# Seven block products in place of eight for the last 8 of the 44 up chunks of a two-layer fp32 transformer kernel

## Chip, cores and metric

One core of one Trainium2 chip runs the whole program once. The metric is the device time of one execution in microseconds, the median of the runs; lower is better. Engine names in the rows: PE is TensorE, PEld its weight loads, DVE VectorE, ACT ScalarE, POOL GpSimd, SP the engine that issues the loads.

## What is computed

Two decoder layers over 512 tokens of width 1024, all in fp32. The change concerns the feed-forward part of the first layer (D_FF is 2816, so `w_up` has 5632 columns, 44 chunks of 128):

```python
def causal_dwconv(x, w, b):            # K = 3 taps over the tokens
    xp = jnp.pad(x, ((0, 0), (K - 1, 0), (0, 0)))
    y = b + xp[:, 0:S] * w[0]
    for j in range(1, K):
        y = y + xp[:, j:j + S] * w[j]
    return y

def conv_ffn(x, w_up, conv_w, conv_b, w_down):
    u = causal_dwconv(x @ w_up, conv_w, conv_b)
    g, val = jnp.split(u, 2, axis=-1)
    return (jax.nn.gelu(g) * val) @ w_down
```

After it come a layer norm, a second layer of mixers and an MLP (`m1`, 1024 to 4096, squared ReLU, and `m2` back).

## The kernel before

**Products.** Each fp32 operand is split into a high and a low half (`whi`, `wlo` for weights, `xh`, `xl` for activations), and each product is three matmuls: high by high, high by low, low by high. A *chunk* is 128x1024 weights (512 KB). Chunks of all weight matrices form one list (`WEIGHTS`, `CHUNKS`): 44 `up` chunks, then 34 `down` chunks, and so on. For each chunk SP loads it into one of 4 `stage` buffers (`NSTAGE`), ACT casts it to `whi`, and DVE subtracts to get `wlo`; the pair lies in one of 7 slots (`NSPLIT`) until PE has used it. A stage buffer is loaded again once the `wlo` of its chunk is done. This is the step `split`; `pump` issues as many as there are slots.

**Order.** A class `Plan` writes one list of steps at build time. Each engine walks that list and issues its own part of each step, in that order; nothing overtakes on an engine. Semaphores count finished work (`mm` chunks multiplied, `w_lo` chunks split, `up_y`, `up_t`, `up_c`, `up_h` stages of the up block, `combined` and `taken` the terms of the block products).

**Up, before.** A plain `up` chunk is 24 matmuls of 512 columns. Chunk `j` is half `r = j % 2` (0 gate, 1 value) of pair `c = j // 2`. ACT copies the bank into `U` (shifted by two tokens) and writes the third tap with the bias (L2234, L2237); DVE adds the other two taps (L2863, L2866); for the gate ACT applies gelu (L2241); for the value DVE multiplies both (L2874) into `hid1`.

**Seven products.** `down`, `m2` and part of `m1` are multiplied in 2x2 blocks with seven products in place of eight (Winograd's form). The products are named `r1`, `r2`, `t11`, `r3`, `t12`, `r4`, `t22`. For `m1`, which computes features as `up` does, a *group* replaces four plain chunks by seven products, each of 24 matmuls of 256 columns. Its sums of activations (`r1` to `r4`) are made once, three of them kept in split slots (so 4 of the 7 slots are left for weights while groups run). The sums of weights (`a` to `d`) are made in DRAM by transfers of GpSimd, 1 MB each, one after the other, each released by a count of chunks (`at(n)` in `add_up`). Between the products of a group come small operations: ACT copies the bank of `r2` (`taken`), DVE makes `v` = that minus `t11`, `w` = `v` plus `r1`, ACT writes `w` back into a bank (`seed`) before `r4` is added there, and DVE makes `c22` and `c21` before `t22` is added. The waits of a product on these:

```python
                if kind == "t12":
                    q.wait_ge(S["combined"], plan.combined_at["m1", "v", g])
                elif kind == "r4":
                    q.wait_ge(S["taken"], plan.copied_at["m1", "seed", g])
                elif kind == "t22":
                    q.wait_ge(S["combined"], plan.combined_at["m1", "c21", g])
```

**Up to down.** The first `down` products need activations made from `hid1`: `x_from("down", k)` is a cast on ACT (`xh`, L2012) and a subtraction on DVE (`xl`, L2525). Those for k = 1 to 3 wait until the first half of chunk 43 is multiplied, those for k = 4 to 6 until `up` is done. A `down` chunk is 12 matmuls of 512 columns.

## Time and profile before

| | us |
|---|---|
| median of 3 runs | 1231.41 (1231.21 to 1232.08) |
| the profiled execution | 1231.81 |
| its span in the trace | 1230.0 |
| PE busy | 1222.7 (99%) |
| DVE busy | 899.3 (73%) |
| ACT busy | 652.9 (53%) |

The span is that of the first to the last instruction; 1.8 us of the profiled time lie outside it. Busy time of PE is modelled from pipelined matmuls, which overlap in the rows (a matmul of 512 columns has a duration of 389 ns, and the next starts 227 ns after it), so a time per chunk is read from starts, not from durations. The same holds for short operations of DVE and ACT, whose next one starts some 0.1 us before the end of the last.

### The profile page before, as it was taken

What the parts mean: (1) busy time and instruction counts of PE and PEld (TensorE: products, weight loads), DVE (VectorE), ACT (ScalarE), POOL (GpSimd) and SP (SyncE); (2) the same over time, 40 slices, a digit from 0 to 9 for tenths busy, and PEclk for the clock granted to TensorE, in tenths of its full rate; (3) what the DMA queues carried; (4) which work ended last, traced back from release to release, by engine and by line L of the source; (5) the groups of instructions that cost most, each with busy time, mean ns of one, the idle gap of its engine ahead of it and who ended that gap; (6) DMA issues with size and microseconds to landing.
All of it is one profiled execution on the core that took longest, in us unless ns stands there. A gap on an engine that the chain in (4) does not pass through costs nothing.

```text
span 1230.0 us, 17180 instructions
## 1 busy us (share of the span) xinstructions
PE 1222.7 (99%) x6662; PEld 1050.5 (85%) x6662; DVE 899.3 (73%) x1281; ACT 652.9 (53%) x1078; POOL 56.0 (5%) x80
## 2 busy tenths in 40 slices
PE   9999999999999999999999999999999999999998
PEld 9887898898889888888888899778898999988886
DVE  6778888576568656555588587887687777887886
ACT  5565654244546444444465464669354544665654
POOL 0000012000000000000000000000000000000000
PEclk9999999999999999999999999999999999999999
DMA  8445478837635787878676429776736789776562
GB/s 296 150 139 192 161 265 226 283 116 210 185 107 188 209 236 208 198 241 202 212 246 181 139 69 259 207 194 191 248 104 159 265 271 265 256 220 190 173 213 78
DMA packets 63976, 244.53 MB, mean 199 GB/s; under 512 B 6900, under 2 KB 14580, under 8 KB 54424
## 3 DMA queue, kind: packets, MB, share of 16 engines
q1 hardware_dynamic: 53096, 167.55, 40.6%
q0 software_dynamic: 10368, 75.50, 24.9%
q8 instruction: 53, 0.87, 0.3%
q10 hardware_dynamic: 432, 0.39, 0.1%
q14 instruction: 27, 0.22, 0.1%
HBM read 235.55 MB, written 81.26 MB: 258 GB/s over the span
## 4 chain that ended last, share of the span: by engine, by line
PE 99%; DMA 0%; DVE 0%; ACT 0%; issue 0%; DVEq 0%
PE bank L1509 15%; PE bank L1510 15%; PE bank L1511 15%; PE bank L1713 6%; PE bank L1715 6%; PE bank L1714 6%; PE bank L1740 3%; PE bank L1741 3%; PE bank L1739 3%; PE bank L1654 2%; PE bank L1658 2%; PE bank L1653 2%; PE bank L1656 2%; PE bank L1655 2%; PE bank L1657 2%; PE bank L1790 1%
## 5 line engine op out<-in xcount | busy, mean ns | idle before, releaser
L2491 DVE TENSOR_TENSOR wlo<-stage,whi 128x1024 fp32r<-128x1024 f32 (+1 forms) x276 | 332.8, 1212 | 113.5 <-ACT whi L1973 112.4
L1509 PE MATMUL bank<-xh,whi 128*128 128x512 f32 (+1 forms) x944 | 339.4, 360 | 0.2 <-issue 0.2
L1510 PE MATMUL bank<-xl,whi 128*128 128x512 f32 (+1 forms) x944 | 335.5, 355 | 0.0
L1511 PE MATMUL bank<-xh,wlo 128*128 128x512 f32 (+1 forms) x944 | 335.5, 355 | 0.0
L1973 ACT CAST whi<-stage 128x1024 fp32r<-128x1024 f32 (+1 forms) x276 | 284.9, 1039 | 78.5 <-PE bank L1715 27.3
L1509 PEld LDWEIGHTS bank<-xh,whi 128*128 128x128 f32 x944 | 178.5, 189 | 29.9 <-issue 5.3
L1511 PEld LDWEIGHTS bank<-xh,wlo 128*128 128x128 f32 x944 | 178.5, 189 | 25.1
L1510 PEld LDWEIGHTS bank<-xl,whi 128*128 128x128 f32 x944 | 178.6, 189 | 24.4 <-issue 0.2
L1715 PE MATMUL bank<-whi,xl 128*128 128x512 f32 x328 | 127.7, 389 | 0.0
L1714 PE MATMUL bank<-wlo,xh 128*128 128x512 f32 x328 | 127.7, 389 | 0.0
L1713 PE MATMUL bank<-whi,xh 128*128 128x512 f32 x328 | 127.7, 389 | 0.0
L1715 PEld LDWEIGHTS bank<-whi,xl 128*128 128x128 f32 x328 | 61.6, 188 | 12.8
L1714 PEld LDWEIGHTS bank<-wlo,xh 128*128 128x128 f32 x328 | 61.6, 188 | 12.8
L1713 PEld LDWEIGHTS bank<-whi,xh 128*128 128x128 f32 x328 | 61.6, 188 | 12.7
L2863 DVE SCALAR_TENSOR_TENSOR R<-R,par 128x512 f32<-128x512 f32 x44 | 33.1, 752 | 53.2 <-ACT R L2237 53.2
L2234 ACT COPY R<-bank 128x512 f32<-128x512 f32 x44 | 25.8, 587 | 82.4 <-PE bank L1511 82.4
L2525 DVE TENSOR_TENSOR xl<-R,xh 128x512 fp32r<-128x512 f32 x92 | 61.7, 686 | 10.5 <-ACT xh L2012 9.6
L2012 ACT CAST xh<-R 128x512 fp32r<-128x512 f32 x70 | 42.4, 616 | 36.2 <-DVE R L3086 20.1
L1741 PE MATMUL bank<-xh,wlo 128*128 128x256 f32 x192 | 54.4, 283 | 0.0
L1739 PE MATMUL bank<-xh,whi 128*128 128x256 f32 x192 | 54.4, 283 | 0.0
L1740 PE MATMUL bank<-xl,whi 128*128 128x256 f32 x192 | 54.4, 283 | 0.0
L2915 DVE SCALAR_TENSOR_TENSOR R<-R,par 128x512 f32<-128x512 f32 x60 | 41.7, 746 | 1.6 <-ACT R L2280 1.3
(408 smaller groups left out, 2017.7 us busy)
## 6 DMA issues: line engine op xcount, KB each, us to landing
stage<-in_W_m SPq DMA_DIRECT2D x50, 512.0 KB, 4.2
stage<-in_W_up SPq DMA_DIRECT2D x44, 512.0 KB, 4.4
m_a<-in_W_m POOLq DMA_DIRECT2D x14, 1024.0 KB, 8.2
m_b<-in_W_m POOLq DMA_DIRECT2D x14, 1024.0 KB, 7.6
stage<-in_W_in_a SPq DMA_DIRECT2D x19, 512.0 KB, 4.4
stage<-in_W_down SPq DMA_DIRECT2D x18, 512.0 KB, 4.3
stage<-in_W_out SPq DMA_DIRECT2D x16, 512.0 KB, 5.3
m_c<-in_W_m POOLq DMA_DIRECT2D x7, 1024.0 KB, 6.1
```

The costliest lines, as they stand in the source:

```text
L1509: e.matmul(b[:, cols], hi[:, k, :], xh[:, k, cols], start=(k == 0), stop=False)
L1510: e.matmul(b[:, cols], hi[:, k, :], xl[:, k, cols], start=False, stop=False)
L1511: last = e.matmul(b[:, cols], lo[:, k, :], xh[:, k, cols], start=False, stop=(k == 7))
L1713: e.matmul(b[:], x[:, c], hi, start=new, stop=False, skip_group_check=True)
L1714: e.matmul(b[:], x[:, c], lo, start=False, stop=False, skip_group_check=True)
L1715: last = e.matmul(b[:], z[:, c], hi, start=False, stop=end, skip_group_check=True)
L1739: e.matmul(o, hi[:, k, w], x[:, k, :], start=(new and f == 0 and k == 0), stop=False, skip_group_check=True)
L1740: e.matmul(o, hi[:, k, w], z[:, k, :], start=False, stop=False, skip_group_check=True)
L1741: last = e.matmul(o, lo[:, k, w], x[:, k, :], start=False, stop=(k == 3), skip_group_check=True)
L1973: e.copy(whi[:, plan.place[i], 0:width(i)], stage[:, s, 0:width(i)]).then_inc(S["w_hi"])
L2491: e.tensor_tensor(wlo[:, plan.place[i], c], stage[:, i % NSTAGE, c], whi[:, plan.place[i], c].bitcast(F32), ALU.subtract).then_inc(S["w_lo"])
L2525: e.tensor_tensor(lo, source_of(name, k), hi.bitcast(F32), ALU.subtract).then_inc(S["x_lo"])
```

## The change

`up` becomes 36 plain chunks and two groups (`g` = 0 and 1) of seven products each, 50 list entries in place of 44. The functions for `m1` get a name as an argument and serve both. Six things change in the order of steps:

- during plain chunks 8 to 15 DVE makes four sums and four differences of the activations; at chunks 32 to 34 three of them are split into high and low and kept in slots;
- within a group ACT evicts three banks into `U` (`up_quarter`), DVE writes the fourth quarter (`c22`);
- the third tap of the values is written after `t22`; the taps, gelu and product of group 0 are issued after `r2` and `t11` of group 1; those of group 1 between the activations for `down` 3 and 4;
- activations for `down` 1 to 3 wait for all of `up` but the last product;
- the transfers that sum weights are 80 in place of 72: 8 for `up` first; from `down` on the list is the old one except that the 8 of the `d` sums of `m2` come last, during `m2`. In `up` one starts every 1.5 chunks (before: every 1.6);
- at the boundary from `out2` to `m1` one of two splits comes after `turn` 2.

```diff
-GROUPS = {"down": 4, "m1": 6, "m2": 8}
+GROUPS = {"up": 2, "down": 4, "m1": 6, "m2": 8}
+UP_PLAIN = 2 * NF1 - 4 * GROUPS["up"]
...
+ORDER = [o for o in ORDER if (o[0], o[2][0]) != ("m2", "d")] + [o for o in ORDER if (o[0], o[2][0]) == ("m2", "d")]
...
             if t == 3:
                 self.used += 5
-                self.pump(2)
+                self.pump(1)
...
             if t >= 2:
                 self.turn(name, t - 1)
+            if t == 3:
+                self.pump(1)
...
-        for j in self.feat("up", 2 * NF1):
-            if j == 2 * NF1 - 1:
-                self.seven_ahead("down")
+        self.up_x = self.x
+        for j in self.feat("up", UP_PLAIN):
...
+            if 8 <= j < 12:
+                self.combine("up", ("t21", "t22", "t11", "t12")[j - 8])
+            elif 12 <= j < 16:
+                self.combine("up", ("r1", "r3", "r2", "r4")[j - 12])
+            elif j == 17:
                 self.seven_first("down")
+            elif UP_PLAIN - 4 <= j < UP_PLAIN - 1:
+                self.sum_kept("up", ("r2", "r1", "r3")[j - UP_PLAIN + 4])
+        for i, (kind, g) in enumerate(FEATS["up"]):
+            self.up_seven(i, kind, g)
...
+    def feat_seven(self, name, i, kind, g, last):
+        if kind not in NEW_BANK:
+            self.fill(name, g, kind)
+        self.need()
+        self.step("seven_feat", name, i)
+        self.used += 1
...
+    def up_seven(self, i, kind, g):
+        last = GROUPS["up"] - 1
+        self.feat_seven("up", i, kind, g, last)
+        if kind == "r2":
+            self.copy("up", "taken", g)
+            self.step("feat_taken", "up", g)
+            if g == 0:
+                self.step("x_sum", "up", "r4")
+                self.x_split("up", "r4")
+            else:
+                self.pump()
+                self.step("up_taps", g - 1, 1)
+                self.step("up_y", g - 1, 0)
+        elif kind == "t11":
+            self.combine("up", "v", g)
+            if g:
+                self.pump()
+                self.up_done(g - 1)
+        elif kind == "r1":
+            self.combine("up", "w", g)
+            self.out(("up", g, "r1"), "combined", self.combined)
+            self.copy("up", "seed", g)
+            self.step("feat_seed", "up", g)
+        elif kind == "r3":
+            self.combine("up", "c22", g)
+            self.combine("up", "c21", g)
+        else:
+            if (kind, g) == ("t22", last):
+                self.seven_ahead("down")
+            n = ("t12", "r4", "t22").index(kind)
+            self.pump()
+            self.step("up_quarter", n, g)
+            self.out(("up", g, ("t11", "r2", "r3")[n]), "up_u", UP_PLAIN + 3 * g + n + 1)
+            if n == 2:
+                self.step("up_y", g, 1)
+                if g == last:
+                    self.step("up_taps", g, 1)
+                    self.step("up_y", g, 0)
+                    self.up_done(g)
+        self.pump()
+
+    def up_done(self, g):
+        self.step("up_taps", g, 0)
+        self.step("up_gelu", g)
+        self.step("up_mult", g)
...
             def x_from(name, k):
-                if name == "down" and k < 4:
-                    q.wait_ge(S["half"], 3)
-                elif name == "m2" and k < 4:
+                if name in SEVEN and k < 4:
                     q.wait_ge(S["mm"], CHUNK0[name] - 1)
...
+            def up_taps(g, r):
+                for i in range(2):
+                    c, u = UP_PLAIN // 2 + 2 * g + i, U[i][r]
+                    y, w = (hid1[:, c, :] if r else ygs[i]), 22 * r + c
+                    q.wait_ge(S["up_y"], UP_PLAIN + 4 * g + (1 if r else 3) + i)
+                    e.scalar_tensor_tensor(out=y, in0=u[:, 0:512], scalar=P("fcw", w), in1=y, op0=ALU.mult, op1=ALU.add
+                                           ).then_inc(own.inc())
+                    after()
+                    e.scalar_tensor_tensor(out=y, in0=u[:, 1:513], scalar=P("fcw", 44 + w), in1=y, op0=ALU.mult,
+                                           op1=ALU.add).then_inc(S["up_t" if r else "up_c"])
...
-                if n < 43:
-                    return CHUNK0["up"] + 2 + 8 * (n - 17) // 5
+                if n < 40:
+                    return CHUNK0["up"] + 2 + 3 * (n - 17) // 2
...
+                return CHUNK0["m2"] + 1 + 4 * (n - 72)
```

What stands in the queue of VectorE over the last plain chunks of `up` before the change (a split, the two tap operations of a chunk, and after each second chunk the product of the pair):

```order
L2491 TENSOR_TENSOR wlo<-stage,whi 128x1024 [waits w_hi,st1]
L2863 SCALAR_TENSOR_TENSOR R<-R,par 128x512 [waits up_y,up_u]
L2866 SCALAR_TENSOR_TENSOR R<-R,par 128x512 [waits v_own]
L2491 TENSOR_TENSOR wlo<-stage,whi 128x1024 [waits w_hi,st2]
L2525 TENSOR_TENSOR xl<-R,xh 128x512 [waits x_hi] x3
L2863 SCALAR_TENSOR_TENSOR R<-R,par 128x512 [waits up_y,up_u]
L2866 SCALAR_TENSOR_TENSOR R<-R,par 128x512 [waits v_own]
L2874 TENSOR_TENSOR R<-R 128x512 [waits up_g,up_t]
L2491 TENSOR_TENSOR wlo<-stage,whi 128x1024 [waits w_hi,st3]
L2525 TENSOR_TENSOR xl<-R,xh 128x512 [waits x_hi]
```

Between the activations of `down` 1 to 3 (the row x3) and that of `down` 4 stand two taps, a product and a split.

The queue of VectorE after the change, from the second tile of group 0's value taps to `w` of group 1. L3168 and L3171 are taps, L3143 is `v` and L3149 is `w` of group 1, L3179 the products of group 0; two splits and two taps stand just ahead of these rows:

```order
L3168 SCALAR_TENSOR_TENSOR R<-R,par 128x512 [waits up_y]
L3171 SCALAR_TENSOR_TENSOR R<-R,par 128x512 [waits v_own]
L3143 TENSOR_TENSOR R<-R,bank4 128x512 [waits taken,mm]
L2587 TENSOR_TENSOR wlo<-stage,whi 128x1024 [waits w_hi,st2]
L3168 SCALAR_TENSOR_TENSOR R<-R,par 128x512 [waits up_y]
L3171 SCALAR_TENSOR_TENSOR R<-R,par 128x512 [waits v_own]
L3168 SCALAR_TENSOR_TENSOR R<-R,par 128x512 [waits up_y]
L3171 SCALAR_TENSOR_TENSOR R<-R,par 128x512 [waits v_own]
L3179 TENSOR_TENSOR R<-R 128x512 [waits up_g,up_t] x2
L3149 TENSOR_TENSOR R<-R,bank7 128x512 [waits combined,mm]
```

All eight taps and both products of group 0 stand ahead of `w` of group 1.

The queue of ScalarE after the change at the same place, from the copy of group 1's `r2` bank (L2136) on; L2156 writes the third tap of the gates, L2162 is gelu, L2140 is the `seed` of group 1:

```order
L2136 COPY R<-bank0 128x512 [waits mm]
L2042 CAST whi<-stage 128x1024 [waits st0]
L2042 CAST whi<-stage 128x1024 [waits st1]
L2156 ACTIVATE R<-R,par 128x512 [waits x_lo,up_h,up_u]
L2156 ACTIVATE R<-R,par 128x512
L2042 CAST whi<-stage 128x1024 [waits mm,st2]
L2162 ACTIVATE R<-R 128x512 [waits up_c] x2
L2140 COPY bank0<-R 128x512 [waits combined]
L2042 CAST whi<-stage 128x1024 [waits mm,st3]
```

The next cast stands behind the `seed`. The queue of VectorE after the change, at the start of `down` (L3159 and L3161 are `c22` and `c21` of group 1, L2621 the activations of `down`); two splits stand ahead of it:

```order
L3159 TENSOR_TENSOR R<-R,bank1 128x2x256 [waits combined,mm]
L3161 TENSOR_TENSOR bank1<-bank1,R 128x512
L2587 TENSOR_TENSOR wlo<-stage,whi 128x1024 [waits w_hi,st1]
L2587 TENSOR_TENSOR wlo<-stage,whi 128x1024 [waits w_hi,st2]
L2587 TENSOR_TENSOR wlo<-stage,whi 128x1024 [waits w_hi,st3]
L2587 TENSOR_TENSOR wlo<-stage,whi 128x1024 [waits w_hi,st0]
L2621 TENSOR_TENSOR xl<-R,xh 128x512 [waits x_hi] x3
L2587 TENSOR_TENSOR wlo<-stage,whi 128x1024 [waits w_hi,st1]
L3168 SCALAR_TENSOR_TENSOR R<-R,par 128x512 [waits up_y]
L3171 SCALAR_TENSOR_TENSOR R<-R,par 128x512 [waits v_own]
```

From there eight taps and two products (L3179) follow before the activation of `down` 4.

## Rows read from the trace of the kernel before

**Rows 1.** The page: span, and busy time of each engine.
```profile
span 1230.0 us, 17180 instructions
PE 1222.7 (99%) x6662; PEld 1050.5 (85%) x6662; DVE 899.3 (73%) x1281; ACT 652.9 (53%) x1078; POOL 56.0 (5%) x80
```
**Rows 2.** Waits of PE, the longest: us in total, times, longest one.
```profile
PE bank L1952 <- DVE R L2564: 1.2, 1, 1.2
```
**Rows 3.** Timeline of ScalarE: start, us, instruction; plain `up`, then `m1` groups.
```profile
597.28 0.59 ACT L2234 COPY R<-bank 128x512 f32<-128x512 f32 x1 [3.24 <-PE bank L1511]
...
608.16 0.59 ACT L2234 COPY R<-bank 128x512 f32<-128x512 f32 x1 [3.24 <-PE bank L1511]
...
953.95 0.59 ACT L2063 COPY R<-bank 128x512 f32<-128x512 f32 x1 [0.30 <-PE bank L1741]
...
974.11 0.59 ACT L2063 COPY R<-bank 128x512 f32<-128x512 f32 x1 [1.35 <-PE bank L1741]
```
**Rows 4.** Windows (last columns: granted clock, DMA share, GB/s): `up`, `m1` groups, `down`.
```profile
569.90:613.40 43.50, 43.50 (x193) 36.05 (x192) 24.57 (x29) 20.88 (x30) 2.96 (x5) 1.00 0.76 217
951.00:1071.60 120.60, 120.60 (x1008) 120.60 (x1007) 93.14 (x110) 65.33 (x81) 5.42 (x8) 1.00 0.83 261
613.40:643.40 30.00, 30.00 (x134) 24.86 (x133) 26.83 (x34) 19.61 (x28) 0.00 (x0) 1.00 0.68 232
```
**Rows 5.** Timeline of VectorE at the end of plain `up`.
```profile
604.09 0.75 DVE L2863 SCALAR_TENSOR_TENSOR R<-R,par 128x512 f32<-128x512 f32 x1 [0.97 <-ACT R L2237]
604.88 0.75 DVE L2866 SCALAR_TENSOR_TENSOR R<-R,par 128x512 f32<-128x512 f32 x1
605.67 0.69 DVE L2874 TENSOR_TENSOR R<-R 128x512 f32<-128x512 f32 x1
606.28 1.22 DVE L2491 TENSOR_TENSOR wlo<-stage,whi 128x1024 fp32r<-128x1024 f32 x1
...
612.79 1.23 DVE L2491 TENSOR_TENSOR wlo<-stage,whi 128x1024 fp32r<-128x1024 f32 x1 [1.71 <-ACT whi L1973]
613.93 1.89 DVE L2525 TENSOR_TENSOR xl<-R,xh 128x512 fp32r<-128x512 f32 x3
```
**Rows 6.** Timeline of ScalarE at the end of plain `up`.
```profile
608.65 0.79 ACT L2237 ACTIVATE R<-bank,par 128x512 f32<-128x512 f32 x1
611.11 0.63 ACT L2241 ACTIVATE R<-R 128x512 f32<-128x512 f32 x1 [1.68 <-DVE R L2866]
611.65 1.03 ACT L1973 CAST whi<-stage 128x1024 fp32r<-128x1024 f32 x1
```
**Rows 7.** Timelines of one `m1` group: `v` and `w` on VectorE, `seed` on ScalarE.
```profile
977.59 0.68 DVE L3044 TENSOR_TENSOR R<-R,bank 128x512 f32<-128x512 f32 x1
978.21 1.23 DVE L2491 TENSOR_TENSOR wlo<-stage,whi 128x1024 fp32r<-128x1024 f32 x1
979.87 0.69 DVE L3048 TENSOR_TENSOR R<-R,bank 128x512 f32<-128x512 f32 x1 [0.44 <-PE bank L1741]
...
980.59 0.59 ACT L2067 COPY bank<-R 128x512 f32<-128x512 f32 x1 [2.49 <-DVE R L3048]
```
**Rows 8.** DMA issues (xcount, KB each, us to landing): page, then window 391 to 613.
```profile
stage<-in_W_up SPq DMA_DIRECT2D x44, 512.0 KB, 4.4
...
stage<-down_c SPq DMA_DIRECT2D x2, 512.0 KB, 6.1
```
**Rows 9.** Timeline, start of `m1`: VectorE's turns 2 and 3, PE's first matmul after.
```profile
911.03 1.28 DVE L2538 TENSOR_TENSOR xl<-bank,xh 128x512 fp32r<-128x512 f32 x2
912.53 1.29 DVE L2538 TENSOR_TENSOR xl<-bank,xh 128x512 fp32r<-128x512 f32 x2 [0.21 <-ACT xh L2045]
...
912.06 0.36 PE L1509 MATMUL bank<-xh,whi 128*128 128x256 f32 x1
```
**Rows 10.** `down` chunk 16: its `v` terms on VectorE, and a matmul at its start.
```profile
654.41 1.28 DVE L3092 TENSOR_TENSOR R<-R,bank 128x512 f32<-128x512 f32 x2 [0.29 <-PE bank L1715]
...
656.93 0.39 PE L1713 MATMUL bank<-whi,xh 128*128 128x512 f32 x1
```

More of the change, by code:

```diff
@@ L125, in feat @@
         for j in range(n):
-            if name != "m1":
+            if name not in PLAINS:
                 x = self.x
@@ L1129, in seven, with sum_kept @@
             self.need(o)
-    def m1_seven(self, i, kind, g):
-        if kind in ("r2", "t11", "r1", "r3"):
-            self.fill("m1", g, kind)
-        self.need()
-        self.step("seven_feat", i)
-        self.used += 1
-        if kind in ("r1", "r2", "r3") and g == NF2 // 4 - 1:
-            self.give(kind, "mm", CHUNK0["m1"] + PLAIN + i + 1)
+    def sum_kept(self, name, kind):
+        self.keep((name, kind))
+        self.step("x_sum", name, kind)
+        self.x_split(name, kind)
@@ new lines, in feat_seven @@
+    def feat_seven(self, name, i, kind, g, last):
[4 more added lines that the diff above has]
+        self.used += 1
+        if kind in ("r1", "r2", "r3") and g == last:
+            self.give((name, kind), "mm", CHUNK0[name] + PLAINS[name] + i + 1)
+    def up_seven(self, i, kind, g):
[38 more added lines that the diff above has]
+        self.pump()
@@ L1377, in build_program @@
         hid2 = tiles(reg(16, NF2 * 512), NF2)
-        rs = {"down": [tiles(reg(60 + 2 * g, 512), 2) for g in range(4)],
+        rs = {"down": [tiles(reg(kb, 512), 2) for kb in (60, 62, 92, 94)],
               "m2": [tiles(reg(92 + 2 * g, 512), 2) for g in range(2)]
@@ L2061, in m1_taken @@
[L2061 to L2067 removed]
+                    q.wait_ge(S["mm"], CHUNK0[name] + PLAINS[name])
+                elif plan.kept[name, kind][1]:
+                    sem, value = plan.kept[name, kind][1]
+                    q.wait_ge(S[sem], value)
@@ new lines, in x_sum, with feat_taken @@
+                e.copy(feat_x(name, kind, 0), raw_of(SUM_AT[kind])).then_inc(S["x_hi"])
+            def feat_taken(name, g):
+                q.wait_ge(S["mm"], CHUNK0[name] + PLAINS[name] + FEATS[name].index(("r2", g)) + 1)
+                if name == "up":
+                    if g >= 2:
+                        q.wait_ge(S["combined"], plan.combined_at["up", "c21", g - 2])
+                    else:
+                        q.wait_ge(S["x_lo"], plan.x_at["up", "r3"])
+                e.copy(feat_v[name][:, g % 2, :], bank_of(name, g, "r2")[:]).then_inc(S["taken"])
@@ L2069, in m1_quarter, with up_gelu @@
+            def up_gelu(g):
+                for i in range(2):
+                    q.wait_ge(S["up_c"], UP_PLAIN // 2 + 2 * g + i + 1)
+                    e.activation(ygs[i], ygs[i], ACT.Gelu_apprx_tanh).then_inc(S["up_g"])
             def m1_quarter(n, g):
-                q.wait_ge(S["mm"], CHUNK0["m1"] + PLAIN + M1_SEVEN.index((("t12", "r4", "t22")[n], g)) + 1)
+                q.wait_ge(S["mm"], CHUNK0["m1"] + PLAIN + FEATS["m1"].index((("t12", "r4", "t22")[n], g)) + 1)
                 e.activation(t_of("m2", ("t11", "t12", "t21")[n], g), tiles(bank_of("m1", g, ("t11", "r2", "r3")[n])[:], 2),
@@ L3056, in m1_last, with up_mult @@
+            def up_mult(g):
+                for i in range(2):
+                    c = UP_PLAIN // 2 + 2 * g + i
+                    q.wait_ge(S["up_t"], c + 1)
+                    q.wait_ge(S["up_g"], c + 1)
+                    e.tensor_tensor(hid1[:, c, :], ygs[i], hid1[:, c, :], ALU.mult).then_inc(S["up_h"])
             def m1_last(g):
```

183 lines of the change are left out of this document (106 added, 77 removed).

## Prediction

> **What bounds the kernel now.** I read the page first: PE is busy 1222.7 of 1230.0 us, VectorE 899.3, ScalarE 652.9 [rows 1]. The list of waits comes next: the longest wait of PE in the whole span is 1.2 us, and that is before the first product [rows 2]. So no engine but PE holds anything up, and every microsecond of matmuls saved is saved at the end, as long as PE never has to wait. For that I read timelines of the two engines that feed PE, and the windows.
>
> **What the products save.** ScalarE evicts every plain `up` chunk as it ends. 597.28 and 608.16 are two chunks apart: 5.44 us a chunk [rows 3]. The copies of the `r2` banks of two following `m1` groups stand at 953.95 and 974.11: 20.16 us for seven products, 2.88 each [rows 3]. Eight plain chunks are 43.52 us, fourteen products 40.32. The change saves **3.2 us**, not an eighth of 43.5: a matmul of 256 columns costs 0.120 us (2.88 / 24), one of 512 columns 0.227.
>
> The Trainium skill (TensorE: Matmul & The Clock Gate, Back-to-back issue gap) gives the gap of two matmuls at the full clock as the columns over 2.4 GHz plus 2.5 ns, 216 and 109 ns. By that rule 8 chunks would be 41.4 us and the fourteen products 36.7, a saving of 4.7 us, and the sum below would end 1.5 us lower. The rows have some 11 ns more at both sizes, and they decide.
>
> **What it adds.** PE takes a product of group 1 only when `v`, `seed` and `c21` are there, and a `down` chunk when its activations are. So I add up the queue of VectorE in order. Its prices are distances of starts: a tap 0.79 (604.09 to 604.88), a 512-column operation 0.61 (605.67 to 606.28), a split 1.14 (612.79 to 613.93), an activation 0.60 [rows 5]; `v` and `w` read a bank at the same 0.61 [rows 7]. On ScalarE a split's cast takes 1.03, a third tap 0.79, a gelu 0.63 [rows 6], a `seed` 0.59 [rows 7], and the next one starts 0.1 before the end. From one engine's end to the next one's start I take 0.06.
>
> Load first. VectorE works 24.57 of 43.50 us beside plain `up`, but 93.14 of 120.60 beside `m1`'s groups, 15.6 of every 20.16 [rows 4]. An `up` group needs seven splits (7.98), four terms (2.44), eight taps (6.32) and two products (1.22): 18.0 of 20.16. That fits on average. But group 0's taps and products can only start in group 1, and those of group 1 fall into the start of `down`, where VectorE is busy 26.83 of 30.00 us already [rows 4]. Group 0 itself is light (10.4 of 20.16), and VectorE can't use the gaps, since only four slots are left for splits.
>
> Let T be the end of group 1's `r2` product. Without waits `r4` would start at T + 11.52 and `t22` at T + 14.40, `down` at T + 17.28.
>
> 1. *Before `r4`.* ScalarE copies the `r2` bank (0.50) and casts a chunk into the slot that `r2` freed (1.04). VectorE starts at T + 1.66. Ahead of `w` lie three splits 3.42, eight taps 6.32, `v` 0.61, two products 1.22 and 0.1 for the last gelu: 11.7. `w` ends at T + 14.0, `seed` at T + 14.7, `r4` starts at T + 14.74. **Wait 3.2 us.** In `m1` the same chain had its `seed` at 980.59 + 0.59 = 981.2 [rows 7], 4.4 us before `r4` (974.11 - 0.06 + 11.52 = 985.6) [rows 3].
> 2. *Before `t22`.* The next cast stands behind `seed` on ScalarE. VectorE gets its chunk at T + 15.68; two splits, `c22`, `c21`: 3.58, ready T + 19.3. `r4` ends at T + 17.6. **Wait 1.7 us.**
> 3. *Before `down` 1.* `down` 0 starts at T + 22.2. Ahead of the activations lie four more splits. Two of them need loads that can only be issued when the splits since T + 15.68 have freed a stage buffer: T + 16.9 plus 4.4 us from issue to landing [rows 8] is T + 21.3, cast and split T + 23.6, one more split T + 25.0, activation T + 25.7. `down` 1 was due at T + 24.9. **Wait 0.9 us.** If the loads land in 3 us it is nothing, and at 6.1 us [rows 8] it is over 2.
> 4. *Before `down` 4.* From T + 25.0: three activations 1.8, a split 1.2, eight taps 6.32, two products 1.3, activation 0.69: T + 36.4. `down` 1 to 3 end at T + 25.8 + 8.16 = T + 33.95. **Wait 2.5 us.** Before, one tap pair and one product stood here.
> 5. *Before `down` 16.* `v` starts at 654.41 and its two take 1.28, and chunk 16 starts at 656.93 [rows 10]: 1.2 us to spare. VectorE still works off its backlog (a `down` chunk has 2.72 us, a split and an activation take 1.74, the `r2` and `r4` terms more), and I get `v` 1.8 us later against PE. **Wait 0.5 us**, the least certain; 0 to 0.6.
>
> Sum of waits: 3.2 + 1.7 + 0.9 + 2.5 + 0.5 = **8.8 us**. If one wait is shorter, the next is longer by about as much, since in all of this stretch VectorE has no pause: the sum is its work. Low end: loads of 3 us and no wait at `down` 16, 6.9. High end: loads of 6.1 us, 10.5.
>
> **What I cost at nothing.** The eight sums of activations (8 x 1.14 = 9.1 us on VectorE) fall into eight plain chunks, where VectorE has 19 idle us in 43.5 [rows 4] and weights lie several chunks ahead; without that cover they would be 9.1. The three kept sums and the one of `r4` (four casts of 0.95 and four splits of 1.14) too: the first to be short is the fourth product's weights, which I get 3.8 us early. Eight more summing transfers run during `m2`, one in four chunks (11 us); `m1` had that pace with DMA busy 0.83 and PE at 120.60 of 120.60 [rows 4]. In `up` one starts every 8.2 us in place of 8.7; should they lag into the groups, they lengthen loads (rival 3). At the start of `m1` the activations of turn 3 are done at 913.8, and PE needs them at 912.06 + 2.88 = 914.9 [rows 9]. The split now ahead of them starts after turn 2's (911.03 + 1.2) and moves them to 914.7: 0.2 us left, so 0 with a bound of 0.3.
>
> **Sum.** 1231.81 - 3.2 + 8.8 = 1237.4 for a profiled execution, whose own time was 0.4 over the median: **1237.0 us**, 0.45% slower.
>
> **Rivals.**
> 1. *The gain is kept* (1228.2). The place is the first ten splits' order: if VectorE had done seven or more of the splits that I put after T + 1.66 in its idle time of group 0, all five waits would go. For it: 9.8 idle us there. Against: a slot is only free when the product four back is done, and the cast of the first of them stands behind the copy of `r2`'s bank. It decides when the waits sum to under 0.7 us. 6%.
> 2. *Only the first wait* (3.2 us) and nothing after, the time as before: 1231.4. It needs VectorE to be 5 us quicker than the rows between T + 15 and T + 36, for instance with shorter taps than 0.79. Nothing in the rows shows that. With all that lies between, 10%.
> 3. *Loads are slow.* If summing transfers or the burst of loads make them 6 to 7 us [rows 8], the same queue gives waits of 10.5 to 13: 1238.7 to 1241. 10%.
> 4. *The clock falls.* PE never waited over 1.2 us [rows 2] and its clock stood at 1.00, 2.4 GHz, in all three windows [rows 4]. A wait of 3.2 us is new. At 1.2 GHz a 512-column matmul needs 213 ns more, a `down` chunk 2.6 us; one to two such chunks give 1240 to 1242. The Trainium skill (TensorE: Matmul & The Clock Gate, HAM oscillation) says that the clock falls to its lower level when the engine idles long enough; no row here shows it. 6%.
> 5. The forecast, 1235.0 to 1238.7: 68%.
>
> Faster by over 0.2% (2.5 us, about what a measurement of this kernel tells from no change) is rival 1, 0.06; within 0.2% is rival 2, 0.10; slower 0.84. The range takes the forecast's bounds, part of what lies below and the nearer half of rival 3: 1234.3 to 1239.6.
>
> **What would show it.** In the profile after: PE 2.88 us a product in both groups; no wait of PE in group 0; waits before `r4` and `t22` of group 1 put down to the `seed` copy and to VectorE, and before `down` 1 and 4 to the activations (L2621); VectorE without a pause for some 20 us there; clock 1.00. Wrong would be: waits summing to under 5 us, a wait in group 0, `m1` or `m2`, or gaps of VectorE in that stretch.

## The result, and the profile after

The changed kernel takes **1242.75 us** (median of 5 runs, 1241.78 to 1244.76) against 1231.41 of the kernel before in the same measurement: 1.0094 times as long, interval 1.0083 to 1.0106. The forecast was 1237.0 with a range to 1239.6. Its page (as [rows 1]), and its waits of PE (as [rows 2]: us in total, times, longest one):

```profile
span 1240.9 us, 17554 instructions
PE 1224.2 (99%) x6806; PEld 1057.1 (85%) x6806; DVE 922.3 (74%) x1307; ACT 662.7 (53%) x1090; POOL 61.6 (5%) x88
```
```profile
PE bank L1783 <- DVE wlo L2587: 4.8, 1, 4.8
PE bank L1808 <- ACT bank L2140: 2.9, 1, 2.9
PE bank L1783 <- DVE xl L2621: 1.3, 1, 1.3
PE bank L2021 <- DVE R L2660: 1.2, 1, 1.2
PE bank L1783 <- DVE R L3217: 0.3, 1, 0.3
```

The second is the wait before `r4` that the prediction names first, the third that before `down` 4, the last that before `down` 16. The longest was not foreseen: it is in `m2`, 477 us later.

How much of the 10.9 us (1240.9 less 1230.0) belongs to which place is read from one instruction that both kernels have: the copy of the `r2` bank in an `m1` group, at 953.95 before [rows 3].

```profile
957.92 0.59 ACT L2136 COPY R<-bank 128x512 f32<-128x512 f32 x1 [0.30 <-PE bank L1810]
```

This row is **3.97 us** later. The other **6.9** arise behind it, at the handover from `m1` to `m2`. The 3.97 are a little too few for what `up` and the start of `down` cost, since the two executions didn't reach `up` at the same time. ScalarE's first copy of `up`, before and after:

```profile
384.78 0.59 ACT L2234 COPY R<-bank 128x512 f32<-128x512 f32 x1 [2.21 <-PE bank L1511]
383.92 0.59 ACT L2329 COPY R<-bank 128x512 f32<-128x512 f32 x1 [2.22 <-PE bank L1584]
```

The 0.86 us between them are scatter of the execution and not the change: `sums_in_down` below has the same instructions up to there and its row stands at 384.66, and all profiled executions lie between 383.92 and 385.26. Counted from this row, `up` and the start of `down` cost **4.83 us**, and 10.9 is 4.83 + 6.93 - 0.86.

**At `up`.** The `r2` copies of groups 0 and 1 stand at 572.10 and 592.29: 20.19 us for seven products, 2.88 each. VectorE from group 1 on, and what PE did:

```profile
603.72 0.68 DVE L3179 TENSOR_TENSOR R<-R 128x512 f32<-128x512 f32 x1
604.56 0.69 DVE L3179 TENSOR_TENSOR R<-R 128x512 f32<-128x512 f32 x1 [0.17 <-ACT R L2162]
605.17 0.68 DVE L3149 TENSOR_TENSOR R<-R,bank 128x512 f32<-128x512 f32 x1
607.55 2.36 DVE L2587 TENSOR_TENSOR wlo<-stage,whi 128x1024 fp32r<-128x1024 f32 x2 [1.70 <-ACT whi L2042]
```
```profile
606.62 0.55 PE L1808 MATMUL bank<-xh,whi 128*128 128x256 f32 x1 [2.88 <-ACT bank L2140]
606.98 0.42 PE L1809 MATMUL bank<-xl,whi 128*128 128x256 f32 x1
607.19 0.41 PE L1810 MATMUL bank<-xh,wlo 128*128 128x256 f32 x1
```

`w` (L3149) ends at 605.85 behind taps and products of group 0, its `seed` follows, and `r4` starts 2.88 us late. Then the matmuls stand 0.21 us apart in place of 0.12: the granted clock had fallen to the lower of its two levels. Windows (columns as in [rows 4]):

```profile
600.00:606.00 6.00, 3.74 (x32) 3.53 (x30) 5.62 (x8) 1.37 (x3) 0.00 (x0) 0.99 0.30 91
606.00:612.00 6.00, 5.38 (x25) 5.41 (x26) 4.45 (x5) 4.29 (x5) 0.00 (x0) 0.50 0.39 113
612.00:618.00 6.00, 6.00 (x38) 5.51 (x38) 5.22 (x7) 5.37 (x8) 0.00 (x0) 0.94 0.83 286
```

A granted clock of 0.50 is 1.2 GHz; PE had idled 2.88 us just before.

**At the handover.** `m1` ends some 4 us later than the 1071.6 of before, and the first chunk of `m2` runs to 1079.1. Ahead of that ScalarE waits for loads (timeline of ScalarE), and PE behind it for what comes of them (timeline of PE):

```profile
1064.88 1.05 ACT L2042 CAST whi<-stage 128x1024 fp32r<-128x1024 f32 x1 [3.69 <-DMA stage<-m_d]
...
1076.30 1.05 ACT L2042 CAST whi<-stage 128x1024 fp32r<-128x1024 f32 x1 [4.94 <-DMA stage<-m_b]
```
```profile
1083.91 0.76 PE L1783 MATMUL bank<-whi,xh 128*128 128x512 f32 x1 [4.78 <-DVE wlo L2587]
```

The issues of the window 1040 to 1080 (columns as in [rows 8]) say why: three summing transfers of 1 MB ran beside these loads. Those of the sums took 6.6 to 9.0 us from issue to landing, in the median of each group (five others, of `in_W_m`, 5.0).

```profile
stage<-m_a SPq DMA_DIRECT2D x3, 512.0 KB, 8.3
stage<-m_b SPq DMA_DIRECT2D x3, 512.0 KB, 6.6
m_a<-in_W_m POOLq DMA_DIRECT2D x1, 1024.0 KB, 11.1
m_b<-in_W_m POOLq DMA_DIRECT2D x1, 1024.0 KB, 10.7
...
m_c<-m_a POOLq DMA_DIRECT2D x1, 1024.0 KB, 10.9
...
stage<-m_d SPq DMA_DIRECT2D x1, 512.0 KB, 9.0
```

In the kernel before the same window has these (the five of `in_W_m`: 3.9); it had issued its last summing transfer at 1037.73:

```profile
stage<-m_a SPq DMA_DIRECT2D x4, 512.0 KB, 4.0
stage<-m_b SPq DMA_DIRECT2D x3, 512.0 KB, 4.8
...
stage<-m_d SPq DMA_DIRECT2D x1, 512.0 KB, 3.1
```

### The profile page after: what moved, and what is told of

It is laid out like the page before. It is cut to its first block, busy times and chain, and to the rows that moved or that the text cites. A ratio compares the mean times of both kernels' runs of the same rounds, so it can differ in the third digit from the quotient of the medians.

```text
span 1240.9 us, 17554 instructions
## 1 busy us (share of the span) xinstructions
PE 1224.2 (99%) x6806; PEld 1057.1 (85%) x6806; DVE 922.3 (74%) x1307; ACT 662.7 (53%) x1090; POOL 61.6 (5%) x88
## 4 chain that ended last, share of the span: by engine, by line
PE 91%; DVE 4%; DMA 2%; ACT 1%; issue 1%; DVEq 0%; ACTq 0%
PE bank L1582 14%; PE bank L1583 13%; PE bank L1584 13%; PE bank L1783 5%; PE bank L1785 5%; PE bank L1784 5%; PE bank L1810 3%; PE bank L1809 3%; PE bank L1808 3%; DVE wlo L2587 2%; PE bank L1724 2%; PE bank L1728 2%; PE bank L1725 2%; PE bank L1727 2%; PE bank L1723 2%; PE bank L1726 2%
## 5 line engine op out<-in xcount | busy, mean ns | idle before, releaser
L1582 PE MATMUL bank<-xh,whi 128*128 128x512 f32 (+1 forms) x880 | 314.2, 357 | 0.2 <-issue 0.2
L1583 PE MATMUL bank<-xl,whi 128*128 128x512 f32 (+1 forms) x880 | 310.3, 353 | 0.0
L1584 PE MATMUL bank<-xh,wlo 128*128 128x512 f32 (+1 forms) x880 | 310.2, 353 | 0.0
L1582 PEld LDWEIGHTS bank<-xh,whi 128*128 128x128 f32 x880 | 166.3, 189 | 27.5 <-issue 5.3
L1584 PEld LDWEIGHTS bank<-xh,wlo 128*128 128x128 f32 x880 | 166.3, 189 | 22.7
L1808 PE MATMUL bank<-xh,whi 128*128 128x256 f32 x256 | 73.9, 289 | 3.1 <-ACT bank L2140 2.9
L1809 PE MATMUL bank<-xl,whi 128*128 128x256 f32 x256 | 73.6, 288 | 0.0
L1810 PE MATMUL bank<-xh,wlo 128*128 128x256 f32 x256 | 73.6, 288 | 0.0
L2621 DVE TENSOR_TENSOR xl<-R,xh 128x512 fp32r<-128x512 f32 x92 | 61.6, 685 | 10.5 <-ACT xh L2079 9.6
L2959 DVE SCALAR_TENSOR_TENSOR R<-R,par 128x512 f32<-128x512 f32 x36 | 27.0, 751 | 37.8 <-ACT R L2332 37.8
L1810 PE MATMUL bank<-whi,wlo 128*128 128x256 f32 x192 | 54.3, 283 | 0.0
```

The lines of the kernel that those rows point to most:

```text
L1582: e.matmul(b[:, cols], hi[:, k, :], xh[:, k, cols], start=(k == 0), stop=False)
L1583: e.matmul(b[:, cols], hi[:, k, :], xl[:, k, cols], start=False, stop=False)
L1584: last = e.matmul(b[:, cols], lo[:, k, :], xh[:, k, cols], start=False, stop=(k == 7))
L1808: e.matmul(o, hi[:, k, w], x[:, k, :], start=(new and f == 0 and k == 0), stop=False, skip_group_check=True)
L1809: e.matmul(o, hi[:, k, w], z[:, k, :], start=False, stop=False, skip_group_check=True)
L1810: last = e.matmul(o, lo[:, k, w], x[:, k, :], start=False, stop=(k == 3), skip_group_check=True)
```

## Experiments

My theories: the cost at `up` is VectorE's queue (A1), with the low clock only taking the place of waits that would have come anyway (A2); the 6.9 us are the three transfers at the handover (A3). Rivals: the low clock has a price of its own; the waits are loads or ScalarE; the handover is disturbed by something the groups leave behind. Medians are of 4 to 12 executions, and shifts are those of one profiled execution. The "shift" is the time of the `m1` row above less 953.95, "net" the same counted from the run's first copy of `up` (so without the scatter ahead of it), the "end" the span less 1230.0. The recorded expectations speak of the shift.

| run | us, median | ratio, interval | shift | net | end |
|---|---|---|---|---|---|
| changed | 1242.75 | 1.0094, 1.0083 to 1.0106 | 3.97 | 4.83 | 10.9 |
| late_sums | 1238.1 | 1.0051, 1.0039 to 1.0064 | 0.05 | 0.01 | 6.3 |
| sums_in_down | 1237.71 | 1.0050, 1.0037 to 1.0062 | 5.94 | 6.06 | 5.9 |
| filler | 1243.11 | 1.0095, 1.0081 to 1.0109 | 4.19 | 4.95 | 12.4 |
| terms_first | 1241.56 | 1.0088, 1.0074 to 1.0102 | 4.64 | 4.20 | 9.3 |
| gap | 1236.67 | 1.0042, 1.0029 to 1.0054 | 4.38 | 4.93 | 4.4 |
| no_taps | 1229.23 | 0.9984, 0.9975 to 0.9993 | -2.47 | -2.03 | -2.5 |
| pool_work | 1239.11 | 1.0063, 1.0050 to 1.0076 | 7.34 | 7.90 | 7.3 |
| mid | 1239.54 | 1.0068, 1.0055 to 1.0082 | 7.25 | 7.30 | 7.7 |
| mid_taps | 1237.6 | 1.0053, 1.0041 to 1.0066 | 5.52 | 5.04 | 5.5 |
| mid_late | 1235.52 | 1.0032, 1.0020 to 1.0044 | 4.89 | 5.29 | 5.5 |
| mid_early | 1231.31 | 1.0003, 0.9994 to 1.0011 | -1.23 | -1.05 | -1.3 |
| mid_clear | 1229.43 | 0.9990, 0.9979 to 1.0001 | -2.35 | -2.13 | -2.4 |

### Which part costs: late_sums, sums_in_down, gap

`late_sums` is the kernel before with the new order and release of the later transfers alone. As in the changed kernel, 11 transfers fewer of the old list run beside `up`; 3 of them go to `m1`, whose transfers then run up to the handover, and 8 to `m2`:

```diff
+ORDER = [o for o in ORDER if (o[0], o[2][0]) != ("m2", "d")] + [o for o in ORDER if (o[0], o[2][0]) == ("m2", "d")]
...
-                if n < 43:
+                if n < 32:
...
-                    return CHUNK0["m1"] + 3 + 2 * (n - 61)
-                return CHUNK0["m1"] + PLAIN + 2 + 4 * (n - 64)
+                    return CHUNK0["m1"] + 2 + 2 * (n - 50)
+                if n < 64:
+                    return CHUNK0["m1"] + PLAIN + 2 + 4 * (n - 54)
+                return CHUNK0["m2"] + 1 + 4 * (n - 64)
```

> The kernel before, all 44 up chunks plain, with only the order and the release of the last summing transfers changed as in the changed kernel: the eight that make the d sums of m2 come last, and from m1's groups to m2 one is released every four products or chunks, so that they run on into m2. Theory A (the delay of 7.0 us between out2 and the end, 10.98 - 3.97 in the two traces, comes from transfers that now run beside the loads at the handover from m1 to m2): the same delay without any up group, 1238 to 1239 us, loads of 8 to 9.5 us just before m2, a wait of PE of 4 to 5 us in m2 on a split of VectorE. Rival B (that delay comes from something the up groups leave behind, or from the split moved at the start of m1): 1231.4 us, as before, and no wait over 1.2 us.

Shift 0.05, end 6.3, and one new long wait of PE (one of 0.5, for `c21` of the last group of `m1`, besides):

```profile
PE bank L1710 <- DVE wlo L2488: 3.9, 1, 3.9
```

So the delay needs no `up` group: A3 as expected, and the rival out.

`sums_in_down` releases sooner:

```diff
-                if n < 58:
+                if n < 44:
+                    return CHUNK0["down"] + 8 + 5 * (n - 40)
...
-                    return CHUNK0["m1"] + PLAIN + 2 + 4 * (n - 62)
+                    return CHUNK0["m1"] + PLAIN + 2 + 4 * (n - 66)
```

> The changed kernel with its summing transfers released sooner: four of the forty-odd early ones go into down, six at m1's groups rather than fourteen are left for the groups, and they end with product 30 of 42, so that none runs at the handover to m2; those of the d sums of m2 stay as they are. Theory A (transfers at the handover cost 7.0 us): 1235 to 1236.5 us, the wait in m2 gone, the wait before r4 of up group 1 still 2.9 us. Rival B (the wait in m2 has another cause): 1242.7 us. Rival C (transfers cost as much wherever they are put, now as longer loads in down or m1): 1239 us or more, with new waits in down or m1.

Nothing is lost behind `m1` (5.94 and 5.9), but the time is 1.2 us over the expected range. The net shift is 1.2 over the changed kernel, and that is one wait: the `v` terms of `down` came 1.4 us late in place of 0.3. The first of the moved transfers had been issued at 639.86, and ahead of these terms ScalarE waited 1.24 us for a load of `down_b` until 648.53 (0.49 for a load in `gap`, which has no transfer there).

The wait before `down` 4 is 1.9 in place of 1.3 as well, but it ends at 628.43, ahead of the first transfer, and `gap` has the same 1.9: no transfer makes it (see `filler`). Theory A for the handover, and for the `v` terms of `down` rival C, as far as one execution shows it: a transfer costs where the stretch beside it has no slack.

`gap` puts no transfer there and leaves `down` free:

```diff
-                if n < 72:
+                if n < 69:
                     return CHUNK0["m1"] + PLAIN + 2 + 4 * (n - 62)
-                return CHUNK0["m2"] + 1 + 4 * (n - 72)
+                return CHUNK0["m2"] + 1 + 4 * (n - 69)
```

> The changed kernel with only the release of the last eleven summing transfers changed: the three that still ran over the last eight products of m1 wait for the start of m2, and the eight of the d sums follow them, one in four chunks. None runs from m1's product 34 to m2, and none is moved into down. Theory A (the three transfers beside the loads at the handover are the whole of the 7.0 us there): no wait over 0.5 us in m2, the shift against the kernel before stays at the 4.0 us that up's end leaves, 1235.0 to 1236.0 us. Rival B (the work is only put off, and transfers in m2 hit loads there): a wait in m2, 1238 us or more.

Eleven transfers now run in `m2`, and no wait is there. Shift 4.38, end 4.4; the median, 1236.67, is 0.7 us over the expected range. In the window 1040 to 1080 the loads take 3.4 to 4.4 us. So three transfers, the first of them released 38 us later (1041.71 in the changed kernel, 1079.43 in `gap`), are the whole of the 6.9 us. A3 is shown.

### What the low clock costs: filler

```diff
+                if (name, kind, g) == ("up", "r4", 1):
...
+                    for _ in range(24):
+                        e.matmul(bank_of("up", 0, "r1")[:, 0:256], first[:, 0, 0:128], first[:, 0, 0:256], start=True,
+                                 stop=True, skip_group_check=True)
```

> The changed kernel with 24 more matmuls of 256 columns, whose product nobody reads, put ahead of r4 of up group 1, where PE waited 2.9 us, so that it has work there. They take 24 x 0.120 = 2.88 us at the full clock, as long as the wait. Theory A (this stretch is bound by VectorE's queue, and PE at the lower clock only used up waits that would have come at t22 and down 1): within 0.6 us of the changed kernel, clock 1.00 from r4 on, and waits before t22 and down 1 of 1 to 2.5 us in sum. Rival B (the fall of the clock has a price of its own, 29 matmuls at 0.213 in place of 0.120 us, 2.7 us): the changed kernel less 2 to 2.7 us.

The clock stayed at 1.00 through the stretch, `r4` came as late, and PE waited elsewhere: 1.5 us before `t22`, 0.3 before `down` 1, 1.9 before `down` 4, 0.3 for `v`.

```profile
603.00:606.00 3.00, 3.00 (x28) 3.00 (x27) 2.75 (x5) 0.76 (x3) 0.00 (x0) 1.00 0.24 97
606.00:609.00 3.00, 2.99 (x26) 2.82 (x25) 1.34 (x2) 3.00 (x4) 0.00 (x0) 1.00 0.00 0
609.00:612.00 3.00, 1.46 (x12) 1.29 (x12) 3.00 (x4) 1.40 (x2) 0.00 (x0) 1.00 0.71 195
```

The net shift is 4.95, against 4.83 with the low clock. `gap` stands between the two: the same wait of 2.88 us before `r4`, but the low clock behind it was shorter (in the changed kernel these three windows have 0.50, 0.50 and 0.87):

```profile
606.00:609.00 3.00, 2.07 (x10) 2.10 (x11) 1.30 (x2) 2.80 (x4) 0.00 (x0) 0.59 0.00 0
609.00:612.00 3.00, 2.78 (x19) 2.61 (x19) 3.00 (x5) 1.60 (x2) 0.00 (x0) 0.84 0.63 193
612.00:615.00 3.00, 3.00 (x26) 2.91 (x25) 2.82 (x3) 2.01 (x3) 0.00 (x0) 1.00 0.77 225
```

Counted from the first copy of `up`, `down` 4 starts at 243.6 us in the changed kernel, 243.7 in `gap` and 243.8 in `filler`, whatever the clock did; PE only waits longer for it, 1.3, 1.9 and 1.9 us. A2 is shown: in this stretch, which VectorE bounds, a slower PE costs nothing. (The filler's whole time is no better since the transfers at the handover are still there, and one wait of 2.4 us in `m2`, with a low clock behind it, came on top: of 12.4 us 8.2 lie behind `up`.) The Trainium skill (TensorE: Matmul & The Clock Gate, HAM oscillation) counts a fall of the clock as lost throughput. At the handover that fits (6.9 us lost for 4.8 of waiting), though no run isolates it there; at `up` this run does not bear it out.

### Whose queue it is: terms_first, no_taps, pool_work

`terms_first` moves the gate taps and products of group 0 behind `c21` of group 1:

```diff
         elif kind == "t11":
             self.combine("up", "v", g)
-            if g:
-                self.pump()
-                self.up_done(g - 1)
...
             self.combine("up", "c21", g)
+            if g:
+                self.up_done(g - 1)
```

> The changed kernel with the gate taps, gelu and products of up group 0 issued after c22 and c21 of group 1 rather than between v and w. Theory A (the sum of the waits is VectorE's work, wherever the taps stand): no wait before r4, one of 3 to 4 us before down 1 and of 2 to 2.5 us before down 4, the time within 1 us of the changed kernel. Rival B (the place of the taps ahead of w is the cost): the 2.9 us before r4 and the low clock behind it go and nothing replaces them, 2.9 to 5.5 us less than the changed kernel.

The wait before `r4` is gone, and one of 3.9 us is there at the start of `down`, on a split:

```profile
PE bank L1782 <- DVE wlo L2586: 3.9, 1, 3.9
```

The net shift is 4.20, 0.6 under the changed kernel, and the median is 1.2 under it, just outside the 1 us. Theory A, though the second wait (before `down` 4) shrank to 0.2 us rather than stay at 2 to 2.5; the low clock behind the first one may have covered it.

`no_taps`, on the base of `gap`, leaves out the taps of the 8 chunks but for 2 columns:

```diff
-                    e.scalar_tensor_tensor(out=y, in0=u[:, 0:512], scalar=P("fcw", w), in1=y, op0=ALU.mult, op1=ALU.add
+                    e.scalar_tensor_tensor(out=y[:, 0:2], in0=u[:, 0:2], scalar=P("fcw", w), in1=y[:, 0:2], op0=ALU.mult, op1=ALU.add
```

> The kernel with the transfers released as in the run gap, and with the sixteen tap operations of VectorE in the two up groups on 2 of 512 columns, so that the convolution of those 8 chunks is left out and some 16 x 0.73 = 11.7 us of VectorE's queue with it; all products, casts and splits stay. Theory A (VectorE's queue makes the waits): none of the waits at r4, down 1, 4 and 16 is left or they sum to under 1 us, the shift after up is -3.2 to -2.2, and the time 1228 to 1229.5 us. Rival B (the waits come from the loads of down, or from ScalarE): 1232 us or more.

The net shift is -2.03: the 3.2 us of the products, less 0.8 at `c21`, for which PE waits 0.6 us (the matmul behind it starts 0.8 later than in an unbroken row), and 0.3 at `down` 1. But for the transfers of `gap` nothing else of the change was touched, so A1 is shown, and so is the saving itself.

```profile
PE bank L2021 <- DVE R L2660: 1.2, 1, 1.2
PE bank L1808 <- DVE bank L3161: 0.6, 1, 0.6
```

`pool_work` takes seven operations off VectorE and gives them to GpSimd:

```diff
+            products(0)
+            for k in (1, 2, 3):
...
+                e.tensor_tensor(tiles(xl[:, k % 8, :], 2), source_of("down", k), tiles(xh[:, k % 8, :], 2).bitcast(F32), ALU.subtract
+                                ).then_inc(S["x_lo"])
+            products(1)
```

> The kernel with the transfers released as in the run gap, and with seven operations of VectorE given to GpSimd, which issues nothing in this stretch: the four products (gate by value) of the two up groups and the activations for down 1 to 3. VectorE's queue loses 4 x 0.61 + 3 x 0.60 = 4.2 us. How long GpSimd takes for a 512-column operation no trace here shows (one of 4 columns takes 1.1 to 2.0 us). Theory A (each us off VectorE's queue is a us less of waits): the run gap less 2 to 4.2 us, about 1232. Rival B (GpSimd is so slow, or slows VectorE so much, that the products come later than now): no gain on gap or a loss, with waits before down 1 or down 4 that end with GpSimd.

Rival B: 2.4 us slower than `gap`. GpSimd takes 1.5 to 1.6 us (3.07 for two, 4.93 for three) for an operation of 0.61 on VectorE, and some operations of VectorE slow down beside it: a split 1.82 in place of 1.22, a tap 1.78 in place of 0.75, an activation 1.71 in place of 0.68. `w`, which takes one operand from a bank, kept its 0.69, and so did two taps (0.75) that had started 0.15 us ahead of GpSimd. The timelines of GpSimd, and of VectorE:

```profile
603.50 3.07 POOL L3467 TENSOR_TENSOR R<-R 128x512 f32<-128x512 f32 x2 [36.06 <-ACT R L2162]
616.11 4.93 POOL L3472 TENSOR_TENSOR xl<-R,xh 128x512 fp32r<-128x512 f32 x3 [9.55 <-ACT xh L2079]
```
```profile
618.06 1.82 DVE L2587 TENSOR_TENSOR wlo<-stage,whi 128x1024 fp32r<-128x1024 f32 x1 [1.77 <-ACT whi L2042]
619.81 1.78 DVE L3172 SCALAR_TENSOR_TENSOR R<-R,par 128x512 f32<-128x512 f32 x1
621.63 0.75 DVE L3175 SCALAR_TENSOR_TENSOR R<-R,par 128x512 f32<-128x512 f32 x1
```

The Trainium skill (GPSIMD Engine Reference, Specifications and Engine selection) says that operations with two inputs are about twice as slow there, and that the interfaces to SBUF, the memory of both, are shared with VectorE, with contention for its operations that have two inputs there. The trace has a factor of 2.5, and the three that slowed down are of that kind.

### Can the gain be had: mid, mid_taps, mid_late, mid_early, mid_clear

If the trouble is that VectorE's backlog of the groups meets the start of `down`, the groups belong further ahead, with plain chunks behind them. `mid` moves them ahead of the last 8 plain chunks. Since plain chunks follow that need the quarter of the activations which `r4`'s sum overwrites, that quarter is copied and restored (`x_back`):

```diff
-UP_PLAIN = 2 * NF1 - 4 * GROUPS["up"]
+UP_LATE = 8
+UP_PLAIN = 2 * NF1 - 4 * GROUPS["up"] - UP_LATE
...
+        for j in self.feat("up", 2 * NF1, UP_PLAIN + 4 * GROUPS["up"]):
...
+            self.step("up", j // 2, j % 2)
...
+                self.step("x_back")
```

> The run gap with the two groups not at the end of up but ahead of its last 8 plain chunks (the groups make pairs 14 to 17, the plain chunks 18 to 21, so the start of down is again the one of the kernel before), and the gate taps and products of group 0 after c21 of group 1 as in the run terms_first. One copy of a quarter of the activations is added (1.1 us on each of ScalarE and VectorE after group 1's r4, 1.1 us of VectorE earlier). Same products, 3.2 us less of PE than before. Theory A (the waits are VectorE's backlog meeting the start of down; with plain chunks behind, of which each leaves VectorE some 2.4 idle us, it is worked off under cover): waits of 0 to 1.5 us in all, 1228 to 1230 us, under the kernel before. Rival B (the groups themselves are too dense for VectorE, 18.0 of 20.16 us, whatever follows): waits of 3 us or more in or just after the groups, 1232 us or more.

A miss, some 10 us over what theory A gave, and in rival B's range: PE waited 7.0 us for the restored quarter, behind four taps, four other operations and three splits of VectorE. Its longest wait of PE, and the end of that queue:

```profile
PE bank L1599 <- DVE xl L2648: 7.0, 1, 7.0
```
```profile
568.45 0.69 DVE L3241 TENSOR_TENSOR R<-R 128x512 f32<-128x512 f32 x1
569.05 0.68 DVE L3243 TENSOR_TENSOR R<-R 128x512 f32<-128x512 f32 x1
569.66 3.49 DVE L2616 TENSOR_TENSOR wlo<-stage,whi 128x1024 fp32r<-128x1024 f32 x3
573.06 1.22 DVE L2648 TENSOR_TENSOR xl<-R,xh 128x1024 fp32r<-128x1024 f32 x1
```

`mid_taps` is `mid` with the taps between `v` and `w` again (the diff of `terms_first` undone).

> The run mid with the gate taps and products of group 0 between v and w of group 1, where the changed kernel has them. Theory A: the wait before r4 of group 1 is there again, 2.9 us, with a low clock behind it (up to 2.7 us), and nothing else; 3 to 5.5 us over the run mid. Rival B (a wait here only stands for a later one, as at the end of up): within 1 us of the run mid.

A miss too: waits of 4.2 us before `r4` and 1.7 for the quarter, 1.9 us faster than `mid`. In both all of group 0's work stands ahead of the quarter; neither order helps while it does.

`mid_late` changes only the order behind group 1's `c21`:

```diff
+        elif g == last:
+            if kind == "r4":
+                self.step("x_back")
+                self.x_split("up", "x21")
...
+            if j == UP_PLAIN + 4 * GROUPS["up"]:
+                self.pump()
+                self.up_rest(GROUPS["up"] - 1)
```

> The run mid with the order behind group 1's c21 changed: the copy that restores the quarter of the activations follows r4 at once, three splits for the plain chunks stand next, and only then come group 0's gate taps and products, the copies of group 1's banks and its taps and products, beside chunks 36 to 38. In the run mid VectorE did four taps, two products, two sums for down and three splits (563.97 to 573.06) ahead of that copy, and PE waited 7.0 us for it. Theory A (what hurts is only which work stands ahead of the operation PE waits for, and plain chunks can take the rest): waits of 0 to 1 us in all, 1228 to 1229.5 us. Rival B (VectorE's work in the groups is too much whatever the order): a wait of 3 us or more for the copy, for c21, or at chunks 37 to 40, 1232 us or more.

Half right. In the groups PE waits 1.6 and 0.3 us and, counted from the first copy of `up`, stands 0.8 us ahead of the kernel before at the end of `up`. But at the start of `down` a split is 3.1 us late, and the clock falls behind it:

```profile
PE bank L1814 <- DVE wlo L2627: 3.1, 1, 3.1
PE bank L1610 <- DVE xl L2659: 1.6, 1, 1.6
```

`mid_early` puts the groups ahead of the last 16 plain chunks (`UP_LATE = 16`), with the quarter restored one split sooner.

> The run mid_late with the two groups ahead of the last 16 plain chunks rather than 8 (pairs 10 to 13), the copy of the activations one split sooner, two summing transfers beside the groups and nine beside the 16 chunks. In the run mid_late PE stood 1.2 us ahead of the kernel before up to the end of up, and lost 6.1 us at the start of down, where a split came 3.1 us late and the clock fell: the last plain chunks' taps and splits still ran behind. Theory A (VectorE's backlog of the groups goes down by about 1 us a plain chunk, so 16 of them clear it): no wait over 1 us at the start of down, PE 1.5 to 3 us ahead from the groups to the end, 1228.5 to 1230.5 us, the first version under the kernel before. Rival B (the start of down waits for loads that the transfers lengthen, not for VectorE): the wait of some 3 us in down is there again, 1234 us or more.

The wait in `down` is gone, as theory A gave it: the backlog needs more than 8 plain chunks. (The last summing transfer of `up` was issued 8 us sooner than in `mid_late`, 597.42 against 605.38, so loads may have had a part in it; this wasn't taken apart.) The net shift is -1.05 and nothing is lost behind it, but the median, 0.8 over the profiled execution, equals that of before and is 0.8 over the expected range. One wait was new:

```profile
PE bank L1844 <- DVE bank L3215: 1.4, 1, 1.4
```

`mid_clear` takes the two transfers beside the groups away:

```diff
-                if n < 31:
-                    return CHUNK0["up"] + 24 + 4 * (n - 29)
+                if n < 38:
+                    return CHUNK0["up"] + 34 + 8 * (n - 29) // 5
                 if n < 40:
-                    return CHUNK0["up"] + 34 + 8 * (n - 31) // 5
+                    return CHUNK0["in2_c"]
```

> The run mid_early with no summing transfer released beside the groups: the two that stood there go behind the others, and the last two of up go to the start of in2. In the run mid_early group 1's t22 waited 1.4 us for c21; the split ahead of it stood behind a cast that waited 1.06 us for its load, and a transfer of 11 us ran beside the loads of the groups (5.9 us to landing in the median). Theory A (that transfer makes the load late): the wait at c21 goes down to some 0.3 us, as in the run mid_late, the span is 1227.2 to 1228.0 us and the median 1229 to 1230.5 us, under the kernel before. Rival B (the wait is VectorE's and the cast's own distance, whatever runs beside): the same 1.2 to 1.7 us wait, 1231.3 us as the run mid_early.

```profile
span 1227.6 us, 17553 instructions
...
PE 1219.8 (99%) x6806; PEld 1054.3 (86%) x6806; DVE 924.6 (75%) x1309; ACT 665.2 (54%) x1091; POOL 61.7 (5%) x88
```
```profile
PE bank L2057 <- DVE R L2710: 1.2, 1, 1.2
PE bank L1844 <- DVE bank L3215: 0.3, 1, 0.3
```

That wait fell to 0.3, and the loads of the window 505 to 530 from 5.9 to 4.4 us, though one transfer that was released earlier still ran there. Wait, span and median are as theory A gave them. The median of 12 executions is 1229.43, 1.8 us under that of before in the same measurement, and 13.3 under the changed kernel. The 12 spread from 1228.27 to 1235.15, and the interval reaches 1.0001: that it beats the kernel before is likely, not shown. Two of them lie above 1231, and what those waited for no profile shows.

## Why the prediction was wrong

**The step that failed** is in "What I cost at nothing": "Eight more summing transfers run during `m2`, one in four chunks (11 us); `m1` had that pace with DMA busy 0.83 and PE at 120.60 of 120.60". I asked what the eight do in `m2`, where no wait of PE followed (nor in `gap`, which has eleven there; `filler` had its one of 2.4 us there, whose cause no run takes apart), and not that three others are pushed back onto the handover. And the row that I took as proof is a mean over 120 us: the last transfer in it was issued at 1037.73, 34 us before `m1`'s end, and the handover itself was free of them. Priced at nothing, it cost 6.9 us, and `late_sums` shows 6.3 of it alone. The chain is: loads of 6.6 to 9.0 us in place of 3.1 to 4.8, casts and splits late, and behind these, in the same queues, the activations of `m2`. A wait in `m2` was one of the prediction's own signs of being wrong.

**The products** save what was forecast: 2.88 us each, and net 2.0 and 2.1 us are left of 3.2 in `no_taps` and `mid_clear`. What is missing is there in late starts of PE, 0.8 + 0.3 in the one and 0.6 + 0.5 in the other.

**Before `r4`**: 3.2 forecast, 2.88 measured; it started 14.4 us after T, 14.74 forecast. The chain was the one written down.

**Before `t22`**: 1.7 forecast, 0.2 measured, since the low clock stretched `r4` over the same time. In `filler`, with the clock up, 1.5 us are there. **Before `down` 1**: 0.9 forecast, none measured, and only 0.3 in `filler`, so this term was too high whatever the clock. **Before `down` 4**: 2.5 forecast, 1.3 measured, 1.9 in `filler`. **Before `down` 16**: 0.5 and 0.3.

**The sum there**: +5.6 forecast, +4.83 measured (net). The excess of 0.8 is no more than what the price of a tap had too much: I took 0.79 from one pair, but in a run of taps the starts are 0.78 and 0.67 apart in turn (596.18, 596.96, 597.63 in the trace after), 0.725 in the mean; for the 16 taps of both groups that is 1.0 us. "The sum is VectorE's work" held within 0.1 us in `filler` and `gap` and within 0.6 in `terms_first`.

**Rivals.** Rival 4, the clock, got 6% and did happen, twice: at `up` for nothing, at the handover for the 2 us or so that the 4.8 us of wait leave of 6.9. I had priced it as an addition wherever it falls. Rival 3 had the right mechanism, loads made longer by summing transfers, and looked for it in `up` alone. The activation sums, the kept sums and the start of `m1` cost nothing, as forecast: no wait of PE stands there. With the transfers kept off the handover the forecast, 5.6 us over the kernel before, would have met `gap`, which is 5.0 over it in its own measurement. Part of that is luck: the waits themselves were further off (8.8 us in all, 6.9 in `filler` with the filled one), and PE's starts came later than its idle time says (4.95 + 3.2 = 8.15). So the forecast missed by 5.7 us because of the 6.9 at the handover, less this excess and the scatter ahead of `up`.

## What to carry to other kernels

When a change pushes background transfers back, list each one's new place against the old and look at every handover it now crosses, in windows of 10 us; a mean over a stage hides the slack that the schedule had there. A stretch that another engine bounds can be shortened by giving it cheap neighbours, not by moving its work within it: here the same products stopped costing time only with 16 plain chunks behind them. Price a low clock by who bounds the stretch.
